# Group B's paged samples: stationary queries and weights in four column tiles, moving keys and values, and a reversed scan for the sums over later tokens

## What is computed

```
z = einsum('nqhd,nkhd->nhqk', q, k) * scale
log_1mb = where(vis, log_sigmoid(-z), 0)        # vis: key position < query position
rev = cumsum(log_1mb, axis=3, reverse=True)
after = concatenate([rev[..., 1:], zeros], -1)   # the sum over later tokens
w = where(vis, exp(log_sigmoid(z) + after), 0)
out = einsum('nhqk,nkhd->nqhd', w, v)
```

## Time and profile before

| | us |
|---|---|
| three runs | 3112.76, 3129.08, 3134.21 |
| their median | 3129.08 |
| the profiled execution: its span | 3141.4 |
| PE matmuls busy in it | 2842.2 (90%) |
| VectorE / ScalarE busy | 1489.0 / 914.1 |

### The profile page before, as it was taken

The page is one execution under the profiler, slowest core; times in us unless marked ns, Lnnn a source line. Parts: engine busy times, 40 slices in busy tenths (PEclk is TensorE's granted clock), DMA queues, the critical chain, the costliest instruction groups (busy, mean ns, idle before and its releaser), DMA issues. The chain is left out here.

```text
span 3141.4 us, 62551 instructions
## 1 busy us (share of the span) xinstructions
PE 2842.2 (90%) x25896; PEld 2665.1 (85%) x25896; DVE 1489.0 (47%) x2600; ACT 914.1 (29%) x1740; POOL 110.2 (4%) x155
## 2 busy tenths in 40 slices
PE   5998999999896898889979989999989959888998
PEld 5998989997785887879979989899977759788997
DVE  5322352225744485973343324421377245769533
ACT  3212252123221253232232224421332214422322
POOL 2100000000000000000001000100000000000001
PEclk7999999999998799989989999999999969999999
DMA  5323324532233122024333133354322422210443
GB/s 175 98 55 79 106 73 138 148 97 72 51 96 101 48 73 93 3 90 134 111 80 88 48 93 93 81 169 131 80 65 59 125 54 62 81 62 3 143 135 130
DMA packets 416914, 284.37 MB, mean 91 GB/s; under 512 B 44701, under 2 KB 386765, under 8 KB 413039
## 3 DMA queue, kind: packets, MB, share of 16 engines
q1 hardware_dynamic: 415710, 269.80, 31.2%
q10 hardware_dynamic: 912, 10.50, 0.9%
HBM read 244.04 MB, written 36.18 MB: 89 GB/s over the span
## 5 line engine op out<-in xcount | busy, mean ns | idle before, releaser
L319 PE MATMUL acc<-h_hi,in_w_hi 128*128 128x272 f32 x3968 | 900.8, 309 | 61.7 <-DVE h_lo L651 35.2
L319 PE MATMUL acc<-h_hi,in_w_lo 128*128 128x272 f32 x3968 | 833.7, 292 | 0.0
L319 PE MATMUL acc<-h_lo,in_w_hi 128*128 128x272 f32 x3968 | 833.6, 292 | 0.0
L319 PEld LDWEIGHTS acc<-h_hi,in_w_hi 128*128 128x128 f32 x3968 | 639.9, 193 | 125.6 <-issue 49.2
L319 PEld LDWEIGHTS acc<-h_lo,in_w_hi 128*128 128x128 f32 x3968 | 638.0, 193 | 0.0
L319 PEld LDWEIGHTS acc<-h_hi,in_w_lo 128*128 128x128 f32 x3968 | 634.6, 193 | 0.0
L349 DVE TENSOR_TENSOR in_w_lo<-in_w_raw,in_w_hi 128x512 fp32r<-128x512 f32 x496 | 349.1, 710 | 509.9 <-ACT in_w_hi L345 507.2
L345 ACT CAST in_w_hi<-in_w_raw 128x512 fp32r<-128x512 f32 x496 | 303.3, 617 | 506.3 <-PE acc L319 369.1
L319 PE MATMUL dr_bank<-over_both,out_weights 128*128 128x272 f32 x1984 | 280.2, 288 | 1.2 <-DVE over_both L690 1.2
L319 PEld LDWEIGHTS dr_bank<-over_both,out_weights 128*128 128x128 f32 x1984 | 260.8, 188 | 1.5 <-DVE over_both L690 1.5
L319 PE MATMUL dr_bank<-out_tiles,out_weights 128*128 128x272 f32 x1088 | 172.3, 294 | 3.8 <-DVE out_tiles L690 3.8
(11 more groups left out here) (396 smaller groups left out, 3427.9 us busy)
## 6 DMA issues: line engine op xcount, KB each, us to landing
in_w_raw<-in_w_in SPq DMA_DIRECT2D x488, 256.0 KB, 2.9
region<-in_cache_sb_kv SPq DMA_DIRECT2D x128, 256.0 KB, 3.1
regions<-in_w_out SPq DMA_DIRECT2D x128, 256.0 KB, 2.8
regions<-in_cache_dsa SPq DMA_DIRECT2D x64, 160.0 KB, 2.2
region<-x_spill SPq DMA_DIRECT2D x32, 272.0 KB, 3.4
x_spill<-region SPq DMA_DIRECT2D x32, 272.0 KB, 2.1
mix_spill<-mix SPq DMA_DIRECT2D x6, 1088.0 KB, 5.4
mix_back<-mix_spill SPq DMA_DIRECT2D x6, 1088.0 KB, 8.7
```

The costliest lines, as they stand in the source:

```text
L319: last = pe.matmul(self.place(i)[:, c, 0:HALF_N], w[:, u % RING, t, :], part[f][:, HALF_N * c:HALF_N * c + HALF_N], start=first and w is k ...
```

## The change

Scores now have (head, sample, query) on the 128 partitions and the 512 past tokens, then the 32 new ones, along the free axis. For a sample and a head the stationary operand is 128x32: its 4 queries among zeros (`queries`, filled by GpSimd, 1 memset and 8 copies), and the moving operand is four pages of keys, 128x512; head h writes PSUM partitions 32h to 32h+31, and the 8 samples accumulate. The ring of transposed keys grows from 4 to 8 pages. A scan along the reversed free axis on VectorE replaces the 15 summing matmuls; 5 transposes then bring the weights back to tokens on partitions. The values are moving (128x128) against 128x32 of stationary weights, again one column tile a head, into two banks that hold every sample's weights times one sample's values; 8 transposes and two additions on VectorE take each sample's own rows out. The yields in the key phase come to 38 units (33 before), in the middle to 12 and 3 (6 and 6), in the value phase to 56 (48).

```diff
+        self.keys = k.R1[:, 4 * NT:4 * NT + 4096].rearrange("p (x h t) -> p x h t", x=8, h=4)
@@ pe
+        quarter = lambda h: slice(NS * h, NS * h + NS)
         for h in range(4):
-            pe.matmul(bank[0:NS, 3, NS * h:NS * h + NS], ft[:, 4 + h, NP:NT], ft[:, h, NP:NT], start=True, stop=True)
+            pe.matmul(bank[quarter(h), 3, 0:NS], ft[:, h, NP:NT], ft[:, 4 + h, NP:NT], start=True, stop=True)
...
-            if u >= 1:
-                s, p = divmod(u - 1, PAGES)
-                pe.wait_ge(self.copied_v if (u - 1) % 2 == 0 else self.copied_s, (u - 1) // 2 + 1)
+            if u >= PAGES and u % PAGES == 0:
+                s = u // PAGES - 1
+                pe.wait_ge(self.copied_v, 2 * s + 2)
+                pe.wait_ge(self.copied_s, 2 * s + 2)
+                pe.wait_ge(self.padded, 1 + NB)
                 for h in range(4):
-                    col = P * p + NS * h + DS * s
-                    last = pe.matmul(bank[:, 2, col:col + DS], self.keys[:, (u - 1) % 4, h, :], ft[:, h, NP + DS * s:NP + DS * s + DS], start=True, stop=True)
+                    last = pe.matmul(bank[quarter(h), 2, :], self.queries[:, s, h, :], self.keys[:, PAGES * (s % 2):PAGES * (s % 2) + PAGES, h, :], start=(s == 0), stop=(s == NB - 1))
                 last.then_inc(self.matched, 1)
-            yield 1
+            yield 2 if u % 8 == 0 else 1
+        yield 12
+        pe.wait_ge(self.exped, 16 + 1)
+        pe.wait_ge(self.left_over, 1)
         for p in range(PAGES):
-            out = bank[:, 0, P * p:P * p + P]
-            pe.matmul(out, k.c("later"), self.miss_s[:, p, :], start=True, stop=False)
-            for q in range(p + 1, PAGES):
-                pe.matmul(out, k.c("ones"), self.miss_s[:, q, :], start=False, stop=False)
-            pe.matmul(out, k.c("ones")[0:NS], new, start=False, stop=True)
-        pe.matmul(bank[0:NS, 1, 0:P], k.c("later")[0:NS, 0:NS], new, start=True, stop=True).then_inc(self.summed, 1)
+            pe.transpose(bank[:, 0, P * p:P * p + P], self.logs_s[:, P * p:P * p + P], k.c("ident"))
+        pe.transpose(bank[0:NS, 1, 0:P], self.logs_s[:, PAST:PAST + NS], k.c("ident")).then_inc(self.turned_w, 1)
+        yield 3
+        pe.wait_ge(self.kept_w, 2)
...
             for h in range(4):
-                last = pe.matmul(bank[:, 3, col:col + DS], self.pages[:, w % RING_P, P * h:P * h + P], self.logs_s[:, p, col:col + DS],
-                                 start=False, stop=(p == PAGES - 1), skip_group_check=True)
+                last = pe.matmul(bank[quarter(h), 2 + s // 4, P * (s % 4):P * (s % 4) + P], self.weights[:, p, quarter(h)], self.pages[:, w % RING_P, P * h:P * h + P],
+                                 start=(p == 0), stop=(p == PAGES - 1))
             last.then_inc(self.consumed, 1)
             if u % 2:
-                yield 3
+                yield 3 + u // 2 % 2
         yield 2
+        pe.wait_ge(self.kept, 5)
+        for b in range(2):
+            pe.wait_ge(self.blocks_kept, b + 1)
+            for s in range(4):
+                last = pe.transpose(bank[:, b, P * s:P * s + P], self.blocks[:, 512 * b + P * s:512 * b + P * s + P], k.c("ident"))
+            last.then_inc(self.blocks_turned, 1)
         meet(pe, self.left, 2)
@@ dve
+        steps.then(dve.tensor_tensor_scan(low[:, ::-1], k.c("ones")[:, 0:1].to_broadcast([P, NT]), miss[:, ::-1], 0.0, ALU.mult, ALU.add))
+        dve.tensor_tensor(log[:, 0:NT - 1], log[:, 0:NT - 1], low[:, 1:NT], ALU.add).then_inc(self.added, 1)
...
+        dve.wait_ge(self.consumed, NB * PAGES)
+        dve.tensor_copy(self.blocks[:, 512:1024], bank[:, 3, :]).then_inc(self.blocks_kept, 1)
+        dve.wait_ge(self.kept, 5)
+        for b in range(2):
+            dve.wait_ge(self.blocks_turned, b + 1)
+            dve.tensor_tensor(self.own_mix(b), self.own_mix(b), self.own_rows(b), ALU.add)
@@ pool
+        pool.wait_ge(self.applied, 4)
+        pool.memset(self.queries, 0.0).then_inc(self.padded, 1)
+        pool.wait_ge(self.padded, 1)
+        for s in range(NB):
+            mine = slice(DS * s, DS * s + DS)
+            pool.tensor_copy(self.queries[:, s, :, mine], self.ft[:, 0:4, NP + DS * s:NP + DS * s + DS]).then_inc(self.padded, 1)
```

More of the change, by code:

```diff
@@ L115, in constants @@
     add("seq_of", (t[:, None] // DS == np.arange(NB)[None]))
-    add("before_s", same & (t[:, None] < t[None]))
+    sample_row = i[:, None] % NS
+    add("earlier_s", (sample_row // DS == t[None] // DS) & (t[None] < sample_row))
     add("dsa_neg", np.where(i[None] <= i[:, None], 0, NEG))
@@ L1329, in __init__ @@
         self.paged, self.turned, self.copied_v, self.copied_s, self.matched = (next(take) for _ in range(5))
-        self.missed, self.summed, self.added, self.left_over, self.consumed = (next(take) for _ in range(5))
+        self.padded, self.masked_s, self.added, self.left_over, self.consumed = (next(take) for _ in range(5))
+        self.turned_w, self.kept_w, self.applied_n, self.blocks_kept, self.blocks_turned = (next(take) for _ in range(5))
         self.loaded = [next(take) for _ in range(RING_P)]
@@ L1336, in __init__ @@
         self.pages = k.R0[:, 0:4096].rearrange("p (a x) -> p a x", x=512)
-        self.keys = k.R0[:, 5120:7168].rearrange("p (x h t) -> p x h t", x=4, h=4)
-        self.logs_s, self.miss_s, self.low_s = (k.R0[:, 7168 + 640 * i:7808 + 640 * i].rearrange("p (g c) -> p g c", g=5) for i in range(3))
+        self.keys = k.R1[:, 4 * NT:4 * NT + 4096].rearrange("p (x h t) -> p x h t", x=8, h=4)
+        self.logs_s, self.miss_s, self.low_s = (k.R0[:, 7168 + NT * i:7168 + NT * i + NT] for i in range(3))
+        self.blocks = k.R0[:, 7168:8192]
+        self.weights = k.R0[:, 5120:5760].rearrange("p (g c) -> p g c", g=5)
+        self.queries = k.R0[:, 8800:9824].rearrange("p (s h c) -> p s h c", s=NB, h=4)
         self.cache = k.cache_sb_kv.rearrange("l n t u h d -> (l n) t u (h d)")
@@ L1343, in blk, with own_rows, own_mix @@
         return t[:, h % 2, self.starts[b] + lo:(self.starts[b + 1] if hi is None else self.starts[b] + hi)]
[L1345 to L1349, removed]
+    def own_rows(self, b):
+        first = self.bank[:, b, NS // 2 * b:NS // 2 * b + 1]
+        return bass.AP(first.tensor, first.offset, [list(first.ap[0]), [P + DS, 4], [NS, 4], [1, DS]])
+    def own_mix(self, b):
+        return self.k.mix[:, 0:4, NP + NS // 2 * b:NP + NS // 2 * b + NS // 2].rearrange("p h (s q) -> p s h q", q=DS)
     def pe(self, pe):
@@ L1421, in pe @@
                 last.then_inc(self.matched, 1)
-            yield 1
[L1423 to L1427, removed]
-        for p in range(PAGES):
-            out = bank[:, 0, P * p:P * p + P]
-            pe.matmul(out, k.c("later"), self.miss_s[:, p, :], start=True, stop=False)
-            for q in range(p + 1, PAGES):
-                pe.matmul(out, k.c("ones"), self.miss_s[:, q, :], start=False, stop=False)
-            pe.matmul(out, k.c("ones")[0:NS], new, start=False, stop=True)
@@ L1437, in pe @@
+        yield 3
+        pe.wait_ge(self.kept_w, 2)
         for h in range(4):
-            pe.matmul(bank[:, 3, NS * h:NS * h + NS], kv[0:NS, QB, 512 + P * h:640 + P * h], self.logs_s[0:NS, 4, NS * h:NS * h + NS],
-                      start=(h == 0), stop=False, skip_group_check=True)
+            last = pe.matmul(bank[:, 0, quarter(h)], kv[0:NS, QB, 512 + P * h:640 + P * h], self.weights[0:NS, 4, quarter(h)], start=True, stop=True)
+        last.then_inc(self.applied_n, 1)
         for u in range(NB * PAGES):
@@ L1499, in act @@
                 act.wait_ge(self.turned, u + 1)
-                if u >= 4:
-                    act.wait_ge(self.matched, u - 3)
-                act.copy(self.keys[:, u % 4, :, :], bank[:, u % 2, :].rearrange("p (h t) -> p h t", h=4)).then_inc(self.copied_s, 1)
+                if u >= 8:
+                    act.wait_ge(self.matched, u // PAGES - 1)
+                act.copy(self.keys[:, u % 8, :, :], bank[:, u % 2, :].rearrange("p (h t) -> p h t", h=4)).then_inc(self.copied_s, 1)
             yield
-        for i, (part, low) in enumerate(zip(self.paged_and_new(self.logs_s), self.paged_and_new(self.low_s))):
-            act.wait_ge(self.lowered, 16 + i + 1)
-            act.activation(part, low, ACT.Abs).then_inc(self.sized, 1)
@@ L1507, in act @@
[L1507 to L1512, removed]
-        yield
-        for i, part in enumerate(self.paged_and_new(self.logs_s)):
-            act.wait_ge(self.added, i + 1)
-            act.activation(part, part, ACT.Exp).then_inc(self.exped, 1)
+        x = self.logs_s
@@ new lines, in act @@
+        act.wait_ge(self.lowered, 16 + 2)
+        act.activation(x, self.low_s, ACT.Abs).then_inc(self.sized, 1)
+        act.wait_ge(self.sized, 16 + 1)
+        act.activation(x, x, ACT.Exp, scale=-1.0).then_inc(self.shrunk, 1)
+        act.wait_ge(self.shrunk, 16 + 1)
+        act.activation(x, x, ACT.Ln, bias=1.0).then_inc(self.opened, 1)
+        yield
+        act.wait_ge(self.added, 1)
```

(48 more changed lines are left out.)

3 lines of the change are left out of this document (removed).

## The result

The changed kernel takes 3058.48 us (median of 6 runs, 3043.46 to 3060.99), the kernel before, timed beside it, 3129.44 (6 runs, 3112.76 to 3141.21). The ratio is 0.9757 [0.9725, 0.9788]: faster, 2.5 us beside the 3061 forecast. The profiled execution took 3043.46 us with a span of 3041.7, so its rows stand for the low end of the runs.

What follows compares the result with a forecast made beforehand. PE was taken to bound the kernel, busy 2842.2 of 3141.4 us. Terms of -16.7, -15.2, -4.35, +0.5 and +1.6 make -34.2 us a layer, -68 in two: span 3073, median 3061, range 3042 to 3104.

Steps and rivals of the forecast that it cites:

- The forecast case: Group B's scores and values: four column tiles run side by side, 1.15 us a sample, 0.75 two pages; chance 0.55.
- The sum: All terms per layer: -34.2 us, -68 in two layers, giving a span of 3073 and a median of 3061.
- tail: At the barrier: 8 transposes and a change of shape, 0.95 us, plus a wait of 0.7; +1.6 together.
- part 1: Scores in the key phase: 25.9 us a layer becomes 9.2 with four tiles side by side, a gain of 16.7.
- Part 2: Value phase: two pages go from 1.70 to 0.75 us, 27.2 to 12.0 a layer, a gain of 15.2.
- The stalls: Key phase: 0.5 us a layer for steps where ScalarE rounds before copying the page a sample's scores need.
- Working in the middle: Between scores and values: an 8.0 us chain to the mask, scan 1.3, hidden behind 12 units with 1.8 to spare.
- From span to median: Whole kernel: the runs' median lies 12.3 us below the profiled span, carried over from 3073 to 3061.
- Half speed: Rival, chance 0.18: only two tiles' streams go at a time in scores and values; 3088 us.
- no overlap: Rival, chance 0.13: column tiles take turns in scores and values; +4.7 us a layer, 3138 us, within 1%.
- Pages late: Rival, chance 0.10: key phase needs 200 GB/s where 182 was the most seen; up to 12 us a layer, 3085.
- Slower by loads that cannot be hidden: Rival, chance 0.04: tiles take turns and each record also costs its weight load; +37 us a layer, 3203 us.

Runs made afterwards that it cites:

- the other two comparisons: The unmodified changed kernel timed twice more beside the kernel before: 3049.78 us (ratio 0.9764) and 3051.08 us (ratio 0.9741).
- The filler of the last experiments: 34 extra fp32 matmuls of 512 columns per layer in PE's idle time late in group C, added to the changed kernel: 3059.01 us, ratio 0.9796.

## Why the prediction was right

*The forecast case.* It named the overlap of four tiles as what everything hangs on, and the runs with one, two and four tiles measured it. 1.15 us for a sample's scores came out as 1.18 and 0.75 us for two pages as 0.79. The step from two tiles to four was an assumption, given 0.55, and it held. Its source was read a little too kindly: half of 52 ns is 26, so the 29 ns of group D's two tiles are 13% above a full overlap, not "fully together". For four tiles the overlap is full, with 0.13 to 0.15 us paid once.

*The sum.* It gave -34.2 us a layer; the units show -39.1. The terms:

| term, us a layer | forecast | measured |
|---|---|---|
| keys, with stalls | -16.2 | -19.0 |
| middle | -4.35 | -4.5 |
| values, whole phase | -15.2 | -16.5 |
| tail | +1.6 | +1.1 |

The term that was mis-sized most is in part 1: the 0.81 us of L1420's 4 matmuls. I subtracted the instruction alone. But four transposes take 0.44 us when L1420 follows them and 0.36 when the stream does (513.75 to 514.11); the unit takes 0.84 behind both. So 2.09 to 1.20 us is 0.89 a step, 0.08 more, times 32. The key step without scores should have been worked out as its own row, transposes followed at once by the stream, and not as the old one less an instruction. Part 2 has the same slip: 1.70 us is the instruction, while the step less its three units is 1.78, 1.3 us a layer in all. (Its 0.75 is a sum of 0.43, 0.22 and 0.08, which is 0.73; 0.3 us a layer.) The stalls (0.5) did not come at all. The table leaves 0.2 us a layer over.

*Working in the middle.* 8.0 us were taken from the scores' end to the mask and 1.3 for the scan of 544 elements. From the row behind the scores (562.41) to 570.21 it is 7.8, and the scan took 1.29; that 1.3 was picked between 0.7 and 1.7, so its closeness is luck. The twelve units hide it with 2.8 us to spare for the 1.8 forecast: the 0.7 for a piece in between did not come.

*From span to median.* I carried 12.3 us over as if it were a constant. The profiled run of the kernel before has the low clock behind group C in both layers, the changed kernel's in none, and there the median lies 15 us above the profiled run and not 12 below. How many a median run has was not traced; the changed kernel's, by their mean clock of 0.946, fit one. The sum was too small by 10 us (68 for 78), and the medians of this comparison differ by 7 us less than the traces' units; the two errors offset each other, so the 2.5 us between forecast and median are in part luck. The 79 and 81 us of the other two comparisons are nearer to what the sum should have given.

*Half speed* (2.0 us a sample, 1.16 for two pages) and *no overlap* (3.64, 1.93): false with four tiles. But with two tiles and with one the kernel behaves much as they priced it: 1.84 and 3.55 us for the scores' records, 1.00 and 1.86 for the values'. The one-tile kernel's 166.9 us against 164.9 is +2.0 a layer for the +4.7 forecast, both within 1%.

*Pages late.* False. Its ceiling of 182 GB/s was the most that rows 2 show, and that was no limit of the transfers: at 237 GB/s PE waits for no page behind the first. Its own counter-argument, the DMA share, was too low as well, 0.80 for 0.70.

*Slower by loads that cannot be hidden.* False. With all heads in one tile, same rows and same columns, a record of 512 takes 0.43 us, from the difference between one tile and two, for the 0.427 by columns: nothing is left for a load, where slower began at 34 ns. The filler of the last experiments bears it out for the full array: 68 records of 512, each with a load of 128 columns, took 29.35 us, 0.43 each. The Trainium skill ("TensorE: Matmul & The Clock Gate", Part 3) says that loads overlap matmuls only where the row group differs; these records share all rows, and the trace does not agree with that sentence (another on the page, that a load may also go ahead into a second weight buffer, it does not contradict). The same part's 2.38 times for three column tiles, by which a sample would take 1.4 us, has no counterpart here: four give 3.55 times and two 1.93, three were not tried.

*Groups C and D* did not take back what B saved.

## What to carry to other kernels

Where a matmul moves few columns against a large stationary tile, turn it round and put independent small outputs into column tiles: with four, fp32, they ran 3.55 times as fast as in turn, and with one the turning alone brought nothing. Count the trips between the stream and the tiles as well (0.36 us each here) and do more on each. When an instruction is taken out of a step, take the new step's length from rows with the same neighbours: the one beside it changes too (0.08 us, 32 times a layer). And before a profiled time is compared with a median, find out which stretch makes the runs differ: two profiles differed here by 100 us, of which the change made 78.

## What was unexpected of the hardware

Behind an idle time of PE of 34 us the granted clock came back to 1.00 within 3.2 us in some runs and stayed at 0.50 for some 33 us in others, with PE full, at a price of 14 to 16 us each; with 5 us of idle time it could still happen. Four column tiles that share every row overlap fully: a record of 512 columns takes 0.43 us of PE in one tile, and four of them together take the same; 0.13 to 0.15 us come on top once, however many records follow. While the pages were moved in the key phase, the core's DMA went to 237 GB/s without a wait for a page behind the first.
